# Ten full-width products on constants in the start-up of a two-layer decoder trunk

## The reference, cut to what matters

```python
mod = jax.nn.silu(c.astype(F32)) @ mod_w[l].astype(F32) + mod_b[l].astype(F32)
sh1, sc1, gt1, sh2, sc2, gt2 = jnp.split(mod[:, None, :], 6, axis=-1)
h = (rmsnorm(x, norm1_g[l]) * (1.0 + sc1) + sh1).astype(dt)
u = h @ w_in[l]
...
```

## Time and profile before

| | us |
|---|---|
| median of three runs | 1583.59 |
| lowest and highest of them | 1581.36, 1586.25 |
| the profiled execution, its own time | 1584.35 |
| its span, first to last instruction | 1582.6 |
| PE busy | 1495.6 (94%) |
| DVE busy | 1074.4 (68%) |
| ACT busy | 816.0 (52%) |
| mean granted clock of TensorE | 0.956 |

### The profile page before, as it was taken

How to read it: one execution, slowest core, us unless ns; L and a number is a source line. 1 busy time by engine, 2 the same in 40 slices (tenths; PEclk the granted TensorE clock), 3 DMA queues, 4 the chain that set the end, 5 groups by cost and what they waited for, 6 DMA issues and landing times.

```text
span 1582.6 us, 22064 instructions
## 1 busy us (share of the span) xinstructions
PE 1495.6 (94%) x8513; PEld 1272.9 (80%) x8513; DVE 1074.4 (68%) x1416; ACT 816.0 (52%) x824; POOL 8.7 (1%) x29
## 2 busy tenths in 40 slices
PE   7989877899999899878999999999999999999997
PEld 4778656899997788767888888888888888888885
DVE  2577212455544783237888888988888888888895
ACT  3233322344432343224666767666677666676763
POOL 1000000000000000000000000000000000000000
PEclk9999889999999999776999999999999999999999
DMA  9942896365554336844979979799798997997960
GB/s 306 296 133 95 287 354 199 116 188 181 167 187 133 134 106 229 259 159 145 336 266 374 379 263 394 272 367 381 256 395 313 326 391 267 373 378 263 394 234 28
DMA packets 259170, 408.30 MB, mean 258 GB/s; under 512 B 9784, under 2 KB 151808, under 8 KB 259104
## 3 DMA queue, kind: packets, MB, share of 16 engines
q1 hardware_dynamic: 243552, 396.67, 71.7%
q10 hardware_dynamic: 15552, 10.74, 2.3%
HBM read 401.49 MB, written 5.95 MB: 257 GB/s over the span
## 4 chain that ended last, share of the span: by engine, by line
PE 82%; DVE 9%; DMA 3%; ACT 3%; SPq 1%; issue 1%; ACTq 0%; DVEq 0%
PE ps L728 19%; PE ps L730 19%; PE ps L729 19%; PE ps L629 5%; PE ps L807 3%; PE ps L717 3%; PE ps L541 2%; PE ps L864 2%; DMA ring<-in_mod_w 2%; DMA out_new_S_sample<-S 1%; PE ps L857 1%; DVE uT L1385 1%; PE ps L616 1%; PE ps L606 1%; DVE ar L1452 1%
## 5 line engine op out<-in xcount | busy, mean ns | idle before, releaser
L1623 DVE TENSOR_TENSOR slab_lo<-ring,slab_hi 128x2048 fp32r<-128x2048 f32 x264 | 604.6, 2291 | 96.0 <-ACT slab_hi L1218 94.5
L1218 ACT CAST slab_hi<-ring 128x2048 fp32r<-128x2048 f32 x261 | 497.9, 1908 | 154.1 <-PE ps L730 154.1
L728 PE MATMUL ps<-slab_hi,tokens_hi 128*128 128x512 f32 (+1 forms) x768 | 301.5, 393 | 2.1 <-DVE slab_lo L1623 2.1
L730 PE MATMUL ps<-slab_hi,tokens_lo 128*128 128x512 f32 (+1 forms) x768 | 288.3, 375 | 0.0
L729 PE MATMUL ps<-slab_lo,tokens_hi 128*128 128x512 f32 (+1 forms) x768 | 286.8, 373 | 0.0
L629 PE MATMUL ps<-hT,ring 128*128 128x264 f32 x768 | 182.4, 398 | 6.4 <-DVE hT L1368 6.4
L629 PEld LDWEIGHTS ps<-hT,ring 128*128 128x128 f32 x768 | 149.6, 197 | 32.7 <-issue 6.9
L728 PEld LDWEIGHTS ps<-slab_hi,tokens_hi 128*128 128x128 f32 x768 | 144.8, 189 | 27.0 <-DVE slab_lo L1623 2.5
L730 PEld LDWEIGHTS ps<-slab_hi,tokens_lo 128*128 128x128 f32 x768 | 145.0, 189 | 26.4
L729 PEld LDWEIGHTS ps<-slab_lo,tokens_hi 128*128 128x128 f32 x768 | 145.2, 189 | 25.6
L1573 DVE TENSOR_TENSOR slab_lo<-ring,slab_hi 128x2048 fp32r<-128x2048 f32 (+1 forms) x34 | 75.7, 2229 | 113.6 <-ACT slab_hi L1159 113.6
(11 more groups left out here) (325 smaller groups left out, 1917.2 us busy)
## 6 DMA issues: line engine op xcount, KB each, us to landing
ring<-in_moe_w SPq DMA_DIRECT2D x264, 1024.0 KB, 6.7
ring<-in_mod_w SPq DMA_DIRECT2D x48, 1024.0 KB, 8.9
ring<-in_ffn_w SPq DMA_DIRECT2D x30, 1024.0 KB, 5.4
ring<-in_w_in SPq DMA_DIRECT2D x24, 1024.0 KB, 5.6
ring<-in_w_out SPq DMA_DIRECT2D x8, 1024.0 KB, 11.9
out_new_S_sample<-S ACTq DMA_DIRECT2D x2, 2048.0 KB, 19.0
ring<-in_ffn_w SPq DMA_DIRECT2D x4, 768.0 KB, 4.2
uT<-in_x_prompt SPq DMA_DIRECT2D x1, 1024.0 KB
```

What stands on the lines that cost most here:

```text
L728: mm(out, x, w, start=start, stop=False)
L730: return mm(out, xl, w, start=False, stop=stop)
L1218: cp(wH[t % 3][:, :], w).then_inc(s_hi, 1)
L1623: tt(wL[t % 3][:, :], w, wH[t % 3][:, :].bitcast(fp32), ALU.subtract).then_inc(s_lo, 1)
```

## The change

DVE first writes 1.0 into 640 words of `ar` that nobody uses yet and raises a new semaphore, `warm_rows`. TensorE waits for it and then runs products of a 128x128 block of these ones with a 128x512 block of them, into `ps[5]`; nobody reads the result. `WARM` says how many stand at each of four places: 6 ahead of the transpose of the condition rows, 1 behind it, 3 between the transposes of the parameter rows and those of x, none ahead of `mean_square`.

```diff
+            def warm(count):
+
+                for _ in range(count):
+                    mm(ps[5][:, :], ar[:, 1536:1536 + P], ar[:, 1024:1536], start=True, stop=True)
+
+            pe.wait_ge(s_warm, 1)
+            warm(WARM[0])
             pe.wait_ge(s_cst, 1)
             pe.wait_ge(s_crow, 16 * 2)
             nc.tensor.transpose(ps[0][:, 0:64 + KC], prow[0:64 + KC, 2, :], ident[0:64 + KC, 0:64 + KC])\
                 .then_inc(s_cT, 1)
+            warm(WARM[1])
             pe.wait_ge(s_cond, 1)
...
             last.then_inc(s_parT, 1)
+            warm(WARM[2])
             pe.wait_ge(s_xrow, 16 * 2)
...
             project(2)
+            warm(WARM[3])
...
+            V.memset(ar[:, 1024:1536 + P], 1.0).then_inc(s_warm, 1)
             dve.wait_ge(s_act0, 1)
...
+WARM = (6, 1, 3, 0)
```

More of the change, by code:

```diff
@@ L324, in trunk @@
         s_fin = sem("final_x")
+        s_warm = sem("warm_rows")
         s_ft = sem("final_transposed")
```

## The result

The changed kernel takes 1577.61 us (median of 16 runs, 1574.48 to 1581.36) against 1583.28 (16 runs, 1574.04 to 1586.25): ratio 0.9966, 95% interval 0.9955 to 0.9977. That is 5.4 us less by the ratio (3.6 to 7.1), where 0.3 was forecast and 1580.4 was the range's lower end. The profiled execution has a span of 1573.5 us, 9.1 less than that of before.

A forecast was written before the change was run, and what follows sets the result against it. TensorE was taken to bound the start-up from x's landing at 15.49 us, capped by slab 7. Shifts of +0.4 and -1.1 us, half weight each, gave -0.35: 1583.59 to 1583.3 us, range 1580.4 to 1587.3.

The forecast's parts named there:

- The late transposes: Start-up: the six first products end at about 9.0 us, so the condition rows' transpose begins 2.0 us late (1.2 to 2.6).
- ACT's own issues as the bound of the slab copies: Start-up: ACT copies slabs 0 and 1 only after its own DMA issues, so faster slab products gain nothing; copies 2.0 us late.
- the clock's fall at 13 to 16 us: Start-up: after 2 us of idleness and 1.5 us of short work, TensorE was expected at half clock again.
- the three products at half clock: Ahead of the x transposes: they take about 4.9 us and end at 21.3, so x begins 5.8 us late.
- chunks of x in under 5 us: Transposes of x: eight chunks take 2.8 us at full clock, 3.2 with the last copy, where 7.1 were needed before.
- the end at slab 7's landing: End of the start-up: slab 7 lands at 36.1 us whatever TensorE does, so the start-up gets at most 1.4 us shorter.
- `mean_square` before: Start-up: 5.1 us with the clock rising inside, 3.56 at full clock; each half the weight for the changed kernel.
- After it nothing of the change is left: Behind the first `w_in` product: no further effect; the start-up's shift of -0.35 us is handed on to the end.
- the prediction's own sign of being wrong: `w_in` before 41 us, x's chunks at 0.8 us again, or the total moving by more than the start does.
- The clock as a matter of luck "by 1 to 2 us": Half-clock stretch behind the idle 2.8 us at 39.68: where the clock moves in it varies between executions by 1 to 2 us.
- The first: Start-up: clock stays up through the gap at 13 to 15 us; -1.4 us (1582.2), extended to 1579.6; chance 0.14.
- The second: Start-up: x's transposes run at half clock all the same; +4.4 us (1588.0), +5.0 with a late first rise; chance 0.17.

The follow-up runs named there:

- e1: The kernel before, unchanged, run and profiled again: ratio 1.0003 to the kernel before.
- e14: The kernel before with only DVE's memset and TensorE's wait for it, no added products: ratio 1.0008.
- e16: The kernel before with the memset, the wait and ten tiny products (40 TensorE instructions) at the start instead of full-width ones: ratio 0.9957 to before.
- e17: Only the three full products ahead of the x transposes, plus 61 tiny ones at the start (256 added instructions in all): ratio 0.9985 to before.
- e5: The kernel before with 16 filler products of 128 columns in TensorE's wait ahead of layer 1's first `w_in` product: ratio 0.9947.
- e9: The kernel before with four filler products after each of three broadcast steps of layer 1 (630 to 636 us): ratio 0.9974.
- e7: The changed kernel with fillers at four places of layer 1, the same as in e6: ratio 0.9931 to the kernel before.
- e8: The changed kernel with only the three products ahead of the x transposes, the first seven left out: ratio 0.9962 to the kernel before.
- e15: The changed kernel with DVE writing 2560 unused words (2.3 us) ahead of the bias, so that `w_in` starts later: ratio 0.9981 to the kernel before.
- e3: The changed kernel without the three products ahead of the x transposes, the first seven kept: ratio 0.9965 to the kernel before.
- e4: The changed kernel with three more products in TensorE's 2.8 us wait ahead of the first `w_in`: ratio 0.9954 to the kernel before.
- e10: The changed kernel with four filler products after each of three broadcast steps of layer 1: ratio 0.9945 to the kernel before.
- e12: The changed kernel with two products of 128 columns (0.45 us) just ahead of layer 1's first `w_in` product: ratio 0.9969 to the kernel before.
- e11: e7 with more fillers, at every wait of known length in the start-up, both layers and ahead of the router: 1563.04 us, ratio 0.9865 to before.
- e6: The kernel before with fillers at four places of layer 1 (ahead of `w_in`, gates, level 5, and after three broadcast steps): ratio 0.9940.

## Why the prediction was wrong, step by step

- **The start-up on TensorE: right in mechanism, wrong in one size.** The late transposes, ACT's own issues as the bound of the slab copies, the clock's fall at 13 to 16 us, the three products at half clock, chunks of x in under 5 us, and the end at slab 7's landing: all of it is in the rows, and `w_in` at 41.06 is 0.2 us under the 41.3 to 42.9 that I had put down for it. x began at 19.55, not 21.3, because the first six products took 6.7 us and not 7.5, the clock having risen some 3 us after they began (6.7 us where full clock takes 5.2), and the three took 3.8 for 4.9. A chunk of x took 0.52 us and not 0.33, 1.3 us more over the eight; that the copies still came in time is luck, since x had begun 1.8 us sooner than forecast. The mis-sized term is `mean_square` before: I took its 5.1 us from one execution, in which the clock had risen early, and weighed a full clock in the changed one at one half. It measured 5.2 to 6.7 us, 6.0 on the mean, in the eight profiles without the three products named under e1, and 3.81 in all ten with them. Start-up: -2.1 us, for -0.35.
- **"After it nothing of the change is left": this step failed.** I let the shift be handed on and everything behind it stay, and the prediction's own sign of being wrong came true: the total moved by more than the start did (5.4 us by the ratio, 1.4 to 2.1 at `w_in`). Behind the start-up stood (1) a fetch of instructions, moved by 40 added instructions off the first packets of a 2 MB store that the feed-forward waits for (0.65 us); and (2) stretches at half clock in layer 1, which became shorter: 1.6 us in the `w_in` products, 1.4 in the gate products and 4.0 in the broadcast stretch. That the number of instructions alone sets this off is shown (e14, e16, e17), and that these stretches are worth the time is shown (e5, e9). That it goes by way of the store is argued from the profiles. The signs of both lie in the trace that I had: the store is in the chain at 223.57, and I had seen the fall at 187.6 with TensorE busy. Nor was the shift handed on whole: of the start-up's 2.1 us, 0.8 are left at 223 us.
- **The clock as a matter of luck "by 1 to 2 us".** The clock's changes aren't fixed to the program, but half-clock stretches drew executions together here: start-ups that end at 42.46, 42.59, 43.92 and 44.84 come to layer 1's `w_in` within 0.8 us, with the same 17.48 us for its products and spans of 1582.0 to 1582.7. A kernel then sits on one side for most of its runs: of the 16 runs of before, 14 took 1580.7 us or more, and of the 16 of the changed kernel 13 took under 1580. I had taken for noise what is largely a property of the kernel.
- **The rivals.** The first (-1.4 to -4.0) had the right sign and the cap by slab 7, but not its cause: in the profile that decides here the clock did fall at 14.8. Whether it falls differs between executions: in e7, e8 and e15 it stayed up, and the three products took 2.7 us. The cap isn't fixed either: slab 7's product waited for its landing until 35.95 in e8 and 36.70 in e7. The Trainium skill's rule that I put beside it ("TensorE: Matmul & The Clock Gate", "Why this matters for your kernels"), that only longer idleness lowers the clock, is contradicted by that fall as by the one at 40.85. The second needed x's chunks at half clock; they ran at 0.52 us a chunk, 4.1 us in all. Part 4 of the same page of the Trainium skill says that transposes don't count as busy for the gate. In before 6.7 us of them raised nothing, and in e3 the clock fell within them, at 16.6, with TensorE busy since 14.94; in the changed kernel it stayed up through 4.1 us of them.
- **The gains don't add.** e16 has only the moved fetch and gains 6.8 us, e17 only the start-up and gains 2.4, the changed kernel has both and gains 5.4 (the intervals of e16 and the changed kernel overlap). Layer 1 has more than two sides: in e4, e8 and e10 its `w_in` products are slow (17.5 us), but the gate products and those behind them near 570 us make it up, so that the slab products come 139.4 us after `w_in`, as in the changed kernel (139.7). Only the broadcast stretch is slow, in e4 and e8. What decides between these is open; e12, meant to test it, came out as the rival had it.

What else stays open: that the six late packets of the store are those of the one DMA engine that also carried the fetch is a guess from their number and time, not shown.

## What to carry to other kernels

- Before a small gain is credited to the edit, add the same number of instructions in a form that does nothing (e16): here that alone was worth as much as the edit, or more.
- TensorE's waits for another engine whose length is known are places for fillers on constants, and not only in the start-up: 1.4% here (e11). The fillers may also make small changes measurable again, though few runs say so: the five of e7 lie within 1.6 us and the four of e11 too, the 16 of the changed kernel within 6.9, but the five of e6 that count within 4.7.
- One profile is one draw of the clock: a term that contains a rise of the clock needs its bounds, not its value.

## What the runs showed that I had not expected

- A single instruction fetch (0.02 MB) that comes 2 or 3 us earlier goes with a 2 MB store of 22.2 us or less instead of 22.7 or more, in all 19 profiles. 40 small instructions that do nothing, which move it, make the kernel 0.4% faster than before (e16); without them nothing is gained (e14).
- The clock falls while TensorE is busy without a gap, on broadcast and one-column products (634.8 us before), and comes back only with the slab products 13.7 us later; with three groups of 0.9 us this stretch is 4 us shorter (e9).
- The profile's clock column shows 1.00 up to the first change that it has recorded, while the rows run at half pace.
